# The pooling stage of a two-layer decoder trunk: separate buffers for groups 0 and 1, gates copied out of PSUM by ScalarE, and a new order of the sample merge

## The reference

```
# pooling, window w of group g (2, 4, 8, 16), 128 channels a group
mean = (sum of the last w rows of pv, the state's 15 rows before them for the samples) / w
y    = (mean - pv) @ pool_w[g] * pool_scale * silu(pg)
b_pool = y @ pool_up
# sample attention: softmax over 8 pages and the new row, then values
o_lat = p @ past_lat + p_new * lat ;  o = o_lat @ w_uv
b_attn = (o * silu(ag)) @ attn_up
sub = (sigmoid(mg_pool) * b_pool + sigmoid(mg_attn) * b_attn) @ w_out
```

## Time and profile before

| | us |
|---|---|
| median of three runs | 2069.68 |
| profiled execution | 2070.5 |
| its span, first to last instruction | 2068.7 |
| TensorE busy (share) | 1926.1 (93%) |
| its weight loads | 1832.6 (89%) |
| VectorE | 916.4 (44%) |
| GpSimd | 727.6 (35%) |
| ScalarE | 555.7 (27%) |
| mean granted clock of TensorE | 0.968 |

### The profile page before, as it was taken

The page is one execution under the profiler, slowest core; times in us unless marked ns, Lnnn a source line. Parts: engine busy times, 40 slices in busy tenths (PEclk is TensorE's granted clock), DMA queues, the critical chain, the costliest instruction groups (busy, mean ns, idle before and its releaser), DMA issues.

```text
span 2068.7 us, 31151 instructions
## 1 busy us (share of the span) xinstructions
PE 1926.1 (93%) x12391; PEld 1832.6 (89%) x12391; DVE 916.4 (44%) x1484; ACT 555.7 (27%) x988; POOL 727.6 (35%) x743
## 2 busy tenths in 40 slices
PE   6999999999998999999979989999999899999994
PEld 5997888888798999999979978888878899999994
DVE  5335566664155111534544546666622831134216
ACT  6132444542121100201341334444511210120002
POOL 2432343341234333444334333343312333334434
PEclk9999999999989999999989999999999899999997
DMA  5214022055612221222131141022474022222212
GB/s 209 76 46 164 23 65 63 24 171 177 227 35 64 72 66 56 87 87 67 46 103 57 39 164 53 30 65 64 154 248 139 23 80 77 70 67 87 67 62 82
DMA packets 94746, 183.96 MB, mean 89 GB/s; under 512 B 12086, under 2 KB 35942, under 8 KB 93964
## 3 DMA queue, kind: packets, MB, share of 16 engines
q1 hardware_dynamic: 73440, 135.43, 21.2%
q10 hardware_dynamic: 21180, 46.80, 6.0%
HBM read 150.19 MB, written 32.45 MB: 88 GB/s over the span
## 4 chain that ended last, share of the span: by engine, by line
PE 72%; DVE 13%; ACT 8%; issue 3%; ACTq 1%; DMA 1%; POOL 1%; DVEq 0%; SPq 0%; POOLq 0%
PE PS L612 50%; PE PS L707 5%; PE PS L635 4%; PE PS L592 4%; DVE MX L1658 3%; ACT PB L1243 2%; ACT PTH L1039 2%; DVE PTL L1646 2%; PE PS L692 2%; PE PS L727 1%; PE PS L668 1%; DVE PS L1657 1%; PE PS L751 1%; PE PS L956 1%; ACT MR L1058 1%
## 5 line engine op out<-in xcount | busy, mean ns | idle before, releaser
L511 POOL CAST WH<-RAW 128x512 fp32r<-128x512 f32 (+3 forms) x292 | 199.5, 683 | 942.7 <-DMA RAW<-in_wstream 942.6
L513 POOL TENSOR_TENSOR WL<-RAW,WH 128x512 fp32r<-128x512 f32 (+3 forms) x292 | 374.0, 1281 | 23.5
L612 PE MATMUL PS<-XH,WH 128*128 128x344 f32 x1344 | 290.9, 325 | 17.0 <-DVEq L1766 16.4
L612 PE MATMUL PS<-XL,WH 128*128 128x344 f32 x1344 | 287.9, 323 | 0.0
L612 PE MATMUL PS<-XH,WL 128*128 128x344 f32 x1344 | 287.0, 322 | 0.0
L612 PEld LDWEIGHTS PS<-XH,WH 128*128 128x128 f32 x1344 | 228.7, 190 | 20.3 <-DVEq L1766 17.5
L612 PEld LDWEIGHTS PS<-XH,WL 128*128 128x128 f32 x1344 | 227.9, 190 | 0.0
L612 PEld LDWEIGHTS PS<-XL,WH 128*128 128x128 f32 x1344 | 227.8, 190 | 0.0
L532 POOL TENSOR_SCALAR PB<-PB,RC 128x128 f32<-128x128 f32 (+7 forms) x128 | 95.6, 747 | 340.2 <-DVE RC L1640 340.2
L635 PE MATMUL PS<-XH,WH 128*128 128x344 f32 x384 | 128.3, 334 | 29.0 <-ACT FST L1039 29.0
L1243 ACT ACTIVATE PB<-PS,NB 128x128 f32<-128x128 f32 (+7 forms) x128 | 94.9, 741 | 188.1 <-DVE NB L1659 187.8
(11 more groups left out here) (273 smaller groups left out, 3886.7 us busy)
## 6 DMA issues: line engine op xcount, KB each, us to landing
RAW<-in_wstream SPq DMA_DIRECT2D x236, 256.0 KB, 2.7
PAGES<-in_pages SPq DMA_DIRECT2D x128, 320.0 KB, 4.9
spill_p<-PST ACTq DMA_DIRECT2D x16, 516.0 KB, 2.9
spill_g<-FST ACTq DMA_DIRECT2D x48, 172.0 KB, 1.9
SGL<-spill_g ACTq DMA_DIRECT2D x16, 516.0 KB, 4.4
PRJ<-spill_p ACTq DMA_DIRECT2D x16, 516.0 KB, 4.3
spill_v<-VSTG ACTq DMA_DIRECT2D x16, 512.0 KB, 2.8
VSP<-spill_v SPq DMA_DIRECT2D x8, 1024.0 KB, 5.3
```

Source lines behind the costliest of these rows:

```text
L511: pool.tensor_copy(WH[:, slot, 0:size], RAW[:, slot, 0:size]).then_inc(w_high[slot], 1)
L513: pool.tensor_tensor(WL[:, slot, 0:size], RAW[:, slot, 0:size], f(WH[:, slot, 0:size]), ALU.subtract).then_inc(w_split[slot], 1)
L612: last = nc.tensor.matmul(PS[:, 3 * par + c, 0:CH], w[:, slot, at], x(k)[:, c * CH:(c + 1) * CH], start=(k == 0 and n == 0), stop=(k == kt ...
```

## The change

Four things are changed together.

1. Buffers. MXF, MXH and MXL become two tensors each, of two slots: groups 0 and 1 use the first (at 12 ROW, where OGL lies), groups 2 and 3 the second. SUMB moves to 10 ROW, where OGH lies. So the sums of groups 2 and 3 no longer wait for mix 0 and mix 1. OGH is written only after the sums of group 3 are done, and OGL after mix 1.
2. Gates. ScalarE copies each gate product from PSUM to SPGB, takes its sigmoid and frees the PSUM set itself; VectorE's gate is a product of two SBUF tensors.
3. TensorE's order: pg 1 goes between the transposition of WS and the small matmuls, mix 0 between the transpositions of PVX and the matmuls with UVF.
4. The orders of VectorE, ScalarE and GpSimd are rewritten to that.

```
-        SUMA, SUMB = at("SUMA", SMALL, ...), at("SUMB", SMALL + 4160, ...)
-        MXH, MXL, MXF = (at(n, SMALL + 8320 + lo, [P, 2, T], dt) for n, lo, dt in (
-            ("MXH", 0, F32R), ("MXL", 2 * ROW, F32R), ("MXF", 2 * ROW, F32)))
+        SUMA, SUMB = at("SUMA", SMALL, ...), at("SUMB", 10 * ROW, ...)
+        MXH, MXL, MXF = ([at(n + "0", 12 * ROW + lo, [P, 2, T], dt), at(n + "1", SMALL + 8320 + lo, [P, 2, T], dt)]
+                         for n, lo, dt in (("MXH", 0, F32R), ("MXL", 2 * ROW, F32R), ("MXF", 2 * ROW, F32)))
...
 GpSimd, for slabs s behind the attention
-                    m = s - slab_of("pg", 2)
-                    if 0 <= m < PAIRS:
-                        pool.wait_ge(og_high, PAIRS * l + m + 1)
-                        pool.tensor_tensor(OGL[:, m, :], ...).then_inc(og_done, 1)
+                    m = s - slab_of("pw", 2)
+                    if s < B_M and 0 <= m < 2:
+                        if m == 0:
+                            products(pool, l, slab_of("pw", 1))
+                        for n in (2 * m, 2 * m + 1):
+                            pool.wait_ge(og_high, PAIRS * l + n + 1)
+                            pool.tensor_tensor(OGL[:, n, :], ...).then_inc(og_done, 1)
...
 ScalarE, pool_gate(g)
                     if g >= 2:
-                        was = slab_of("pg", g - 2)
-                        act.wait_ge(unit_free[par_of(was)], q_of(l, was) + 2)
-                    nc.scalar.activation(thirds(SGB[:, g % 2, :]), bank_set(par_of(s)), ACT.Sigmoid).then_inc(sg_ready, 1)
+                        act.wait_ge(h_done, 4 * l + g - 1)
+                    copy(thirds(SPGB[:, g % 2, :]), bank_set(par_of(s)))
+                    nc.scalar.activation(thirds(SGB[:, g % 2, :]), bank_set(par_of(s)), ACT.Sigmoid
+                                         ).then_inc(unit_free[par_of(s)], 1)
...
 VectorE, gated(g)
-                    dve.wait_ge(sg_ready, 8 * l + 4 + g + 1)
-                    own(v.tensor_tensor(thirds(SPGB[:, g % 2, :]), bank_set(par), thirds(SGB[:, g % 2, :]), ALU.mult))
-                    dve.sem_inc(unit_free[par], 1)
+                    dve.wait_ge(unit_free[par_of(s)], q_of(l, s) + 2)
+                    own(v.tensor_tensor(SPGB[:, g % 2, :], SPGB[:, g % 2, :], SGB[:, g % 2, :], ALU.mult))
...
 VectorE's order behind WS
+                mixed(0, POOL_WINDOWS[0])
+                mix_low(0)
+                mixed(1, POOL_WINDOWS[1])
+                mix_low(1)
+                (WNS and SELW)
+                gated(0)
+                mixed(2, POOL_WINDOWS[2])
+                gated(1)
+                (OLT)
+                mixed_product(0)
+                (OT)
+                mix_low(2)
+                mixed(3, POOL_WINDOWS[3])
+                mix_low(3)
+                mixed_product(1)
+                gated(2)
+                gated(3)
+                mixed_product(2)
+                mixed_product(3)
```

More of the change, by code:

```diff
@@ L961, in _ @@
                 last.then_inc(pvt_done, 1)
+                mix_unit(0)
                 pe.wait_ge(aux_in, 32 * l + 32)
@@ L969, in _ @@
                 last.then_inc(os_done, 1)
[L971 to L975, removed]
+                gate_unit(2)
+                mix_unit(1)
+                gate_unit(3)
+                mix_unit(2)
+                mix_unit(3)
                 pe.wait_ge(og_done, PAIRS * (l + 1))
@@ L1307, in _ @@
                     copy(OGH[:, m, :], OT[:, m, :]).then_inc(og_high, 1)
[L1308 to L1313, removed]
+                pool_gate(2)
+                product_copy(1)
+                pool_gate(3)
+                product_copy(2)
+                product_copy(3)
                 act.wait_ge(h_done, 4 * l + 4)
@@ L1711, in _ @@
                 last.then_inc(wn_ready, 1)
[L1712 to L1718, removed]
-                    last = v.tensor_copy(OLT[:, k, :, :].rearrange("p h b -> p b h"),
-                                         PS[:, 7, k * 64:(k + 1) * 64].rearrange("p (b h) -> p b h", h=N_HEADS))
-                last.then_inc(olt, 1)
-                dve.wait_ge(os_done, l + 1)
-                for half in range(2):
-                    lo, hi = 64 * half, 64 * half + 64
-                    src = PS[lo:hi, 7, 2 * P:2 * P + 64].rearrange("p (i x b) -> p i x b", i=PAIRS, x=2)[:, :, half, :]
-                    last = v.tensor_tensor(OT[lo:hi, :, SEQ:T], src, OT[lo:hi, :, SEQ:T], ALU.mult)
-                last.then_inc(s_done, 1)
                 own.end()
-                own = steps(1 + 2 + 3 + 4 + 4 * 3 + 4)
-                dve.wait_ge(s_done, l + 1)
+                own = steps(1 + 1 + 2 + 3 + 4 + 4 * 3 + 4)
                 for b in range(2):
@@ L1788, in _ @@
                 mixed(0, POOL_WINDOWS[0])
-                gated(0)
-                mix_low(0)
-                for g in range(4):
-                    if g < 3:
-                        mixed(g + 1, POOL_WINDOWS[g + 1])
-                        gated(g + 1)
-                        mix_low(g + 1)
-                    mixed_product(g)
+                mix_low(0)
+                mixed(1, POOL_WINDOWS[1])
+                mix_low(1)
+                dve.wait_ge(wn_done, l + 1)
+                own(v.tensor_copy(WNS[:], PS[:, 6, 2 * P:2 * P + DEC]))
+                for b in range(DEC):
+                    last = v.tensor_scalar(SELW[:, b, :], SEL[:], WNS[:, b:b + 1], None, ALU.mult)
+                last.then_inc(selw_ready, 1)
+                gated(0)
+                mixed(2, POOL_WINDOWS[2])
+                gated(1)
+                dve.wait_ge(olt_done, l + 1)
+                for k in range(KC):
+                    last = v.tensor_copy(OLT[:, k, :, :].rearrange("p h b -> p b h"),
+                                         PS[:, 7, k * 64:(k + 1) * 64].rearrange("p (b h) -> p b h", h=N_HEADS))
+                last.then_inc(olt, 1)
+                mixed_product(0)
+                dve.wait_ge(os_done, l + 1)
+                for half in range(2):
+                    lo, hi = 64 * half, 64 * half + 64
+                    src = PS[lo:hi, 7, 2 * P:2 * P + 64].rearrange("p (i x b) -> p i x b", i=PAIRS, x=2)[:, :, half, :]
+                    last = v.tensor_tensor(OT[lo:hi, :, SEQ:T], src, OT[lo:hi, :, SEQ:T], ALU.mult)
+                last.then_inc(s_done, 1)
+                mix_low(2)
[6 more added lines that the diff above has]
+                mixed_product(3)
                 own.end()
```

33 lines of the change are left out of this document (18 added, 15 removed).

## The result

| | before | after |
|---|---|---|
| median | 2067.54 us (2061.49 to 2071.45, 4 runs) | 2045.34 us (2043.03 to 2047.89, 4 runs) |
| profiled execution, its span | 2070.5, 2068.7 | 2043.62, 2041.8 |
| mean granted clock | 0.968 | 0.975 |

The ratio is 0.9895, 95% interval 0.9866 to 0.9925: faster by 1.05%, 22 us. The forecast was 2050 us, 4.7 us above the median.

The account below looks back on a forecast made before the run. TensorE's idle time (12.3 us per layer) and low clock bound the stage before the merge. Gains of 9.6 us per layer, 19.3 in all, took 2070.5 to 2051.2; the median, 0.8 lower, gave 2050 us, range 2042 to 2060.

Parts of the forecast that it names:

- Step 1: VectorE's wait for transposed WS: sums 0 and 1 go there at no cost; SELW covered by 5.3 us.
- Step 2: TensorE: gate product 1 directly follows the transposition of WS, 0.3 us behind, taking 11.5 us at full clock.
- Step 3: TensorE's small matmuls, mix 0 and UVF: clock falls a few microseconds in; 10.3 us, between 6.7 and 13.2.
- Step 4: Before gate product 3: a 4.2 us wait for ScalarE's PSUM release, OGH copies queued ahead of gate 2.
- sums 3 clean: Sign of wrong size: group 3's sums take 7.5 us, without the 2 us charged for GpSimd's pieces.
- Step 5: Gate product 3 to OGH: 11.5 + 1.9 us for lost clock, then 4.8 us; contention could add 2.4 us.
- Step 6: GpSimd: OGL moves behind mix 1, attention weights split 2 us later, by 637; cost 0, cover 4 us.
- The sum: Per layer: OGH starts 8.7 us earlier, plus 0.9 us of clock in the merge, 9.6 us; both layers 19.3.
- Rival B: Small matmuls: the clock never falls, VectorE then sets the chain; 2044 to 2048 us, chance 0.15.
- Rival C: VectorE and GpSimd block each other in sums 3 and the gate product: 4.4 us per layer, 2059 us, chance 0.15.
- D: Behind the stage: the gain is lost because weight stream or SGL loads start no earlier; 2069 us, chance 0.04.
- E: Gate products 2 and 3: the clock stays low, OGH starts 5.8 us later than now; 2082 us, chance 0.06.

Follow-up runs that it names:

- Experiment 5: Changed kernel with gate product 1 and mix 0 back behind UVF on TensorE, VectorE's and ScalarE's steps with them: 2076.3 us, ratio 1.0064 to the kernel before.
- experiment 1: Changed kernel with the four OGH copies moved behind gate product 2's copy and sigmoid on ScalarE: 2041.8 us, ratio 0.9881 to the kernel before.
- experiments 1 and 2: The second: changed kernel with VectorE again multiplying the gates from PSUM and freeing the set, ScalarE only taking the sigmoid: 2053.63 us, ratio 0.9948.
- experiment 10: The changed kernel unaltered, run again beside the others as yardstick: 2046.67 us, ratio 0.9901 to the kernel before.
- experiments 6 and 7: Changed kernel reordered, SELW matmuls spread inside gate product 2 (2040.76 us) or in one block behind it (2036.8 us).
- experiment 9: Spread kernel with OGL 0 and 3 on VectorE, OGL 0 in its wait for a ScalarE copy, 3 behind gate 2: 2039.38 us, ratio 0.9877.

## Why the prediction was right, and where it was off

- **Step 1 (sums in VectorE's wait).** Right, with less cover: SELW was ready at 589.3, 4.0 us before TensorE asked for it, where 5.3 were summed. The transposition of WS came 1.2 us earlier in this execution (581.60 against 582.83), so SELW was 1.2 us late against the sum, most of it in its own eight operations, which took 2.43 us instead of 1.17. In layer 1 the cover was 4.3 us. Experiment 5 shows that the cover is gate product 1: without it the wait is 7.24 us.
- **Step 2.** Right: gate product 1 started 0.15 us behind the transposition and ended at 593.2, 11.5 us later at full clock.
- **Step 3.** Summed 10.3 us, measured 9.7 in layer 0 (593.23 to 602.97) and 11.0 in layer 1, both inside 6.7 to 13.2. The clock fell 4.1 and 2.6 us in, as I had supposed without a row for it, and stayed low through UVF.
- **Step 4, the term that was mis-sized.** The mechanism was right: one wait, ended by ScalarE's sigmoid, with the OGH copies ahead of it, and experiment 1 shows that cause. Its size was 2.24 us (2.01 in layer 1), not 4.2, and so below the 3 to 6 us that I had named as the sign of being right; "sums 3 clean", named as a sign of a wrong size, is what happened. Sums 3 lasted 7.16 us, not 9.5, because GpSimd's pieces fell just before and just behind them (604.04, 613.70); MXL 2 lost 0.9 us instead. In the four profiled executions with this order of VectorE (the changed kernel twice, experiments 1 and 2) sums 3 lasted 7.2 us in seven of eight layers and 9.7 in one, layer 1 of experiment 10. The charge of 2 us was thus wrong as a mean: it falls due when a piece of the weight stream meets the sums, as it did once in eight.
- **Step 5.** Gate product 3 took 13.0 us (13.4 summed), and from mix 2 to OGH 5.0 (4.8 summed). The gate on the path took 1.24 us. The rule that I weighed against the change holds: the Trainium skill, SBUF — State Buffer, section Who interferes with whom, says that a VectorE instruction with two SBUF inputs contends with a GpSimd one that reads SBUF; here gate 2, beside OGL, took 3.42 us. Gate 2 was off the path because ScalarE had freed PSUM before.
- **Step 6.** Right: OGL ran from 619.4 to 631.7, the attention weight was split by 633.6, cover 4.7 us. That this cover is thin is what experiments 6 and 7 ran into.
- **The sum.** The distance fell by 11.1 and 9.7 us, where 8.7 were summed: the shorter wait, and in layer 0 also the clock that held through the 32 small matmuls, which is luck of that execution (layer 1 took 1.2 us more for step 3). OGH began 56.7 and 58.1 us behind the transposition, 57 to 61 forecast. The clock at the merge was kept whole (1.3 us, 0.9 summed). The two stages give 20.8 us, the medians 22.2.
- **Rival B** (the clock never falls in the small matmuls) did not occur in the changed kernel as written. Nearest comes layer 1 of experiment 10, where the clock fell but was back before UVF, with the consequence that B named: VectorE's chain sets the end. Its price was wrong there. The layer was slower than its neighbour, by 2.6 us, since sums 3 met both GpSimd pieces. **Rival C** (VectorE and GpSimd block one another) occurred there in part, in sums 3 (2.5 us over clean); gate 3 took 1.23 to 1.24 us in all four layers of the changed kernel. **D** did not occur: 641 to 800 is busy for 159.00 of 159.00 us. **E** did not: the clock was back 5 us after UVF ended and 4 us after gate 3 began.

What stays open: what makes executions differ by up to 8 us outside the stage, of which the other 3.3 us between the stages of the profiled pair are a part, and whether the two clusters of experiment 9 are the same thing. The early sums and ScalarE's release were not run each by itself on the kernel before, so their single shares are known only as what the changed kernel loses without them.

## What to carry to other kernels

When work moves into an engine's idle time, find for each engine the instruction at which its queue stands while the others wait: here TensorE's order alone lost half a per cent, the early sums, buffers and PSUM release without that order lost as much, and all together gained 1%, because each removed the wait that the next would have become. An engine that frees a shared resource should have as little as possible queued ahead of the release; moving one release ahead of four copies was worth 3 us a layer. And price a two-input SBUF operation of VectorE by what GpSimd does at that moment, 1.2 or up to 3.4 us, even in idle time. Last, where executions differ by more than the effect, compare a distance inside the stage and not the medians.

## What the hardware showed

- Small matmuls follow the clock in full: 32 on SELW took 3.63 us at 2.4 GHz and 6.97 at 1.2 GHz (113 and 218 ns each), 16 on UVF 1.85 and 3.5 us.
- Spread four at a time between groups of 344-column matmuls, the same 32 left the granted clock at 1.00 in all six layers; in one block, with TensorE busy throughout, it fell 2.5 to 4.3 us behind the start of the first of them.
- Where the clock falls and returns around the small matmuls varies in the same order of work. The 32 on SELW took 3.63 to 4.55 us, and in one of eight layers, in four executions of kernels with this order and no wait ahead of UVF, the clock was back at 2.4 GHz before UVF.
- VectorE's 128x1032 operation with both inputs in SBUF took 1.22 to 1.24 us undisturbed, and 2.2 to 2.4, 3.42 and 3.44 beside GpSimd's subtractions of weights and of OGL; with one input in PSUM the gate took 1.22 to 1.23 us each time; a tail of 128x16 elements took 1.26 us instead of 0.17.
